# A streaming encoder layer on 8 cores: another order of loads in the head, and w_o and w_pgate loaded in pairs

## The chip, the cores and the metric
The kernel runs on all 8 cores of one Trainium2 chip, each with its own prompt sequence and its own share of the sample streams, with no exchange between cores. The time is the device time of the slowest core, in microseconds, as the median of several runs.

## The reference, cut to what matters
```python
h = rmsnorm(x, g_pre)
xa, ba, ca, za, xb, zb, ga, gb = split(h @ w_in)          # 8 sections of 1024 columns
conv = conv_b + sum(conv_w[k] * shifted(ca * xa, k) for k in range(3))
ya = ((ba * conv) * silu(za)) @ w_a_out
d  = trailing_mean(xb) - xb                               # windows 2, 4, 8, 16, by channel group
yb = ((d @ w_grp) * pool_scale * silu(zb)) @ w_b_out
m  = sigmoid(ga) * ya + sigmoid(gb) * yb
x1 = x + rmsnorm(m @ w_o, g_post)
out = x1 + (p @ w_ple) * sigmoid(x1 @ w_pgate)
```
D is 1024. A core has 2176 rows: 2048 of one prompt and 128 of four sample streams. The last rows of ca * xa and of xb are returned as well.

## The kernel before, in words
The rows are cut in tiles of 128. The first half H1 is tiles 0 to 7 (two blocks of 512 rows), the second half H2 is tiles 8 to 16 (two blocks of 512 and the sample block of 128). Each half passes through three stages.

In the first stage (P1) j runs over eight groups of 128 channels. For each j and block `p1_conv` makes four projections (xa, ca, ba, za) and `p1_pool` two (xb, zb). One projection of a block, a group (line 604), is eight matmuls of 128x128 weights against 512 columns of the transposed normed rows, which lie in hA for H1 and in hB for H2. The xb weight is multiplied with w_grp beforehand (`fold`, line 745), from a transposed copy w_xbt, two j at a time (jp). In the second stage (P2, `p2_unit`) each j and block needs four groups: ga and gb from hA or hB, then w_a_out times vT, then w_b_out times qT; their combination m goes to mT by an addition on GpSimd (line 811). The third stage (P3, `p3_tile`) multiplies tiles of m by w_o and of x1 by w_pgate; H1's P3 tiles run within H2's first stage.

Weights come from HBM in float32 and are written as bfloat16 by loads that GpSimd issues (line 595, the POOL queue), 524 KB read and 256 KB written each. They use six slots w of their own and, during H1's first stage, nine more in mT (called mT in the profile). x tiles are loaded by SyncE (lines 908 and 552, the SP queue), 512 KB each, into slots which lie in the later homes of w_o and w_pgate (called wo and wpg in the profile). In the head the SP queue holds x0, the row g_pre (line 909), x1 to x3, the small tensor sml, and x4 to x7. The POOL queue holds four weights of j = 0, four of j = 1 (after tile 0's power), two w_xbt tiles and w_grp, the fifth weights of j = 0 and 1, and the next w_xbt tiles.

A loaded x tile in the head is squared and summed on ScalarE (line 555), scaled (line 557), raised to -1/2 on GpSimd (line 559), multiplied by the statistic and g_pre on VectorE in two halves (line 562, tile hb), transposed by eight TensorE matmuls (line 575) and copied into hA (line 579). g_pre is broadcast over the partitions by two float32 matmuls with a matrix of ones (line 912), from a row in vT that is cleared ahead (line 468), and copied to gbc (line 914). While it has nothing to do in the head, TensorE multiplies the identity by itself (line 491, the filler), up to a planned 12.5 us. For j = 0 the projections of a block run tile by tile, 128 columns each; for j = 1 a block at once.

w_o and w_pgate are sixteen loads by GpSimd (line 1017), after all norms of both halves, since they overwrite the x slots. They have no slot to wait for.

What sets the order: the program records operations with an engine, a duration, a key and their dependences. `Plan.schedule` simulates the engines and the two DMA queues with these durations and the constant DMA_RATE, and takes on each engine, at each moment, the ready operation of the lowest key. From this comes a fixed order of instructions on every engine, in which each instruction waits for its semaphores. On the chip a waiting instruction holds up all that stand behind it on its engine.

## Time and profile before
| | |
|---|---|
| median of 3 runs | 759.61 us (759.2 to 760.65) |
| the profiled execution | 759.77 us |
| its span on the slowest core | 758.2 us (other cores from 756.5) |
| TensorE busy | 745.3 us, 98% |
| VectorE / ScalarE / GpSimd busy | 384.3 / 254.3 / 339.8 us |
| HBM read / written | 117.35 / 11.36 MB |

The span is from the first to the last instruction of a core. A busy TensorE is one on which a matmul is in flight, whether it is useful work or filler. DMA issues are listed by the engine that issues them, with the time from issue to landing.

### The profile page before, as it was taken

How to read it: one execution, taken by the hardware profiler on the slowest of the kernel's cores; microseconds unless marked ns; L12 is line 12 of the kernel's file. 1: busy time of each engine (PE TensorE's matmuls, PEld its weight loads, DVE VectorE, ACT ScalarE, POOL GpSimd, SP SyncE). 2: the span in 40 equal slices, each digit the busy share in tenths (PEclk: the TensorE clock that was granted, in tenths of full speed). 3: DMA queues.
4: the chain of work that ended last, by engine and by line, in shares of the span. 5: the costliest groups of instructions: out<-in, count | busy, mean ns of one | idle time of the engine just before them, and what ended most of it. 6: DMA issues, size and time to landing. Idle time of an engine off the chain costs nothing.

```text
span 758.2 us, 13217 instructions; the slowest of 8 cores (756.5 to 758.2 us)
## 1 busy us (share of the span) xinstructions
PE 745.3 (98%) x4386; PEld 376.5 (50%) x4386; DVE 384.3 (51%) x639; ACT 254.3 (34%) x514; POOL 339.8 (45%) x514
## 2 busy tenths in 40 slices
PE   6899999999999999999999999999999999999998
PEld 5665454444444444454545545455455555555444
DVE  4775667776622112455557666575751212224655
ACT  3533444442211111333333333343421111115453
POOL 5333555558642433342435536466582342211544
PEclk9999999999999999999999999999999999999999
DMA  8999769858995564827547384474747354306643
GB/s 184 219 149 195 92 156 167 155 109 130 172 156 78 75 92 61 139 76 138 87 85 129 78 135 79 90 132 63 152 84 119 56 80 63 55 0 202 157 119 125
DMA packets 65907, 87.82 MB, mean 116 GB/s; under 512 B 30897, under 2 KB 34737, under 8 KB 65842
## 3 DMA queue, kind: packets, MB, share of 16 engines
q0 software_dynamic: 29792, 50.41, 45.1%
q1 hardware_dynamic: 36050, 36.57, 17.4%
...
HBM read 117.35 MB, written 11.36 MB: 170 GB/s over the span
## 4 chain that ended last, share of the span: by engine, by line
PE 93%; DMA 4%; POOL 1%; DVE 1%; issue 1%; ACT 0%; SPq 0%; DVEq 0%; ACTq 0%; POOLq 0%
PE ps L604 74%; PE ps L829 8%; PE ps L876 7%; DMA w<-w_in 2%; PE ps L882 2%; DMA wo<-x 2%; PE ps L745 1%; PE ps L575 0%; PE ps L781 0%; POOL sp L713 0%; POOL mT L595 0%; DVE hb L562 0%; DVE sg L894 0%; ACT hb L555 0%; DVE qT L897 0%
## 5 line engine op out<-in xcount | busy, mean ns | idle before, releaser
L604 PE MATMUL ps<-hB,w 128*128 128x512 bf16 (+1 forms) x912 | 156.5, 326 | 0.0
L604 PE MATMUL ps<-hA,w 128*128 128x512 bf16 (+1 forms) x816 | 143.6, 329 | 2.6 <-DVE hA L579 1.9
L604 PEld LDWEIGHTS ps<-hB,w 128*128 128x128 bf16 x912 | 77.1, 98 | 72.0
L604 PE MATMUL ps<-hB,hA 128*128 128x512 bf16 (+1 forms) x624 | 108.6, 326 | 0.0
L604 PEld LDWEIGHTS ps<-hA,w 128*128 128x128 bf16 x816 | 69.2, 98 | 69.0 <-issue 3.7
L808 DVE SCALAR_TENSOR_TENSOR tA<-tA,ps 128x512 f32<-128x512 f32 (+1 forms) x40 | 24.3, 609 | 141.5 <-PE ps L604 141.5
L604 PE MATMUL ps<-hA,mT 128*128 128x512 bf16 x400 | 91.4, 379 | 0.0
L811 POOL TENSOR_TENSOR mT<-tA,tB 128x512 bf16<-128x512 f32 (+1 forms) x40 | 44.0, 1109 | 84.4 <-DVE tB L808 84.0
L604 PEld LDWEIGHTS ps<-hB,hA 128*128 128x128 bf16 x624 | 52.8, 98 | 49.1
L805 ACT ACTIVATE tA<-ps 128x512 f32<-128x512 f32 (+1 forms) x40 | 21.3, 533 | 152.3 <-PE ps L604 147.5
L876 PE MATMUL ps<-wpg,x1T 128*128 128x512 bf16 (+2 forms) x296 | 61.7, 362 | 0.0
L713 POOL TENSOR_TENSOR sp<-sp 128x524 f32<-128x524 f32 (+5 forms) x60 | 59.5, 992 | 4.8 <-DVE U L658 1.0
L604 PEld LDWEIGHTS ps<-hA,mT 128*128 128x128 bf16 x400 | 38.7, 98 | 45.4 <-issue 0.4
L829 PE MATMUL ps<-wo,mT 128*128 128x512 bf16 x272 | 60.8, 379 | 0.0
L604 PE MATMUL ps<-qT,w 128*128 128x512 bf16 (+1 forms) x272 | 56.4, 351 | 0.0
L699 POOL COPY X<-ptail 128x15 f32<-128x15 f32 x32 | 10.4, 325 | 98.5 <-PE ps L604 98.5
L595 POOL DMA_DIRECT2D w<-w_in x75 | 41.4, 553 | 28.0 <-PE ps L604 24.3
L713 POOL TENSOR_TENSOR sp<-X 128x526 f32<-128x526 f32 (+1 forms) x40 | 42.3, 1058 | 20.6 <-ACT X L701 20.3
L670 ACT ACTIVATE tB<-U,sml 128x512 f32<-128x512 f32 (+1 forms) x40 | 29.9, 749 | 62.2 <-DVE U L661 58.9
L604 PE MATMUL ps<-vT,w 128*128 128x512 bf16 (+1 forms) x224 | 47.8, 356 | 0.0
L876 PEld LDWEIGHTS ps<-wpg,x1T 128*128 128x128 bf16 x296 | 28.3, 98 | 30.5
L829 PEld LDWEIGHTS ps<-wo,mT 128*128 128x128 bf16 x272 | 26.6, 98 | 31.8
...
## 6 DMA issues: line engine op xcount, KB each, us to landing
w<-w_in POOLq DMA_DIRECT2D x75, 256.0 KB, 7.3
hA<-w_in POOLq DMA_DIRECT2D x26, 256.0 KB, 8.0
hA<-x SPq DMA_DIRECT2D x10, 512.0 KB, 3.5
y<-hA SPq DMA_DIRECT2D x10, 512.0 KB, 3.8
mT<-w_in POOLq DMA_DIRECT2D x19, 256.0 KB, 8.7
wo<-x SPq DMA_DIRECT2D x9, 512.0 KB, 8.2
wpg<-x SPq DMA_DIRECT2D x8, 512.0 KB, 13.9
w<-w_b_out POOLq DMA_DIRECT2D x14, 256.0 KB, 5.5
```

Source lines behind the costliest of these rows:

```text
L595: w_op = OP('pool', lambda e, d: d(e.dma_start(out=w.ap[:], in_=src)), 0.56, key, ins=list(rd), opens=[w], dma=mb, after=after, tag=name, ...
L604: ins_ = e.matmul(bk.ap[:, parts[0]:parts[1]], lhsT=w.ap[:, kk, :], rhs=act(kk), start=(kk == 0), stop=(kk == 7))
L670: OP('act', lambda e, d: d(e.activation(out=cv(), in_=win(U.ap, k, 2, 2, 2 + Es), func=AF.Identity, bias=cw(3), scale=cw(2))), act_us(N, 2 ...
L699: OP('pool', lambda e, d: d(e.tensor_copy(out=X.ap[:, 1:16], in_=ptail[:, j, :])), 0.24, ke - 1.0, ins=[tx], opens=[X], after=[gops[0]], t ...
L713: d(e.tensor_tensor(out=win(nxt.ap, k, 16, nlo, E), in0=win(cur.ap, k, 16, nlo, E), in1=win(cur.ap, k, 16, nlo - w, E - w), op=ALU.add))
L745: ins = e.matmul(bk.ap[:, i * 128:(i + 1) * 128], lhsT=wt[cb].ap[:, kk, :], rhs=wgrp[:, jp, cb, c * 128:(c + 1) * 128], start=(cb == 0), s ...
L805: OP('act', lambda e, d, t=t, g=g: d(e.activation(out=t.ap[:, 0:N], in_=bks[g].ap[:, 0:N], func=AF.Tanh, scale=0.5)), act_us(N), ke + g8 * ...
L808: OP('dve', lambda e, d, g=g: d(e.scalar_tensor_tensor(out=tt[g].ap[:, 0:N], in0=tt[g].ap[:, 0:N], scalar=1.0, in1=bks[2 + g].ap[:, 0:N], ...
L811: OP('pool', lambda e, d: d(e.tensor_tensor(out=mT[:, j, k.rel:k.rel + N], in0=tt[0].ap[:, 0:N], in1=tt[1].ap[:, 0:N], op=ALU.add)), pool_ ...
L829: ins = e.matmul(ob[h].ap[:], lhsT=mT[:, kk, tl.rel:tl.rel + 128], rhs=wo[:, kk, h * 512:(h + 1) * 512], start=(kk == 0), stop=(kk == 7))
L876: ins = e.matmul(bg.ap[:, 0:n], lhsT=x1T.ap[:, kk, :], rhs=wpg[:, kk, sl], start=(kk == 0), stop=(kk == 7))
L882: ins = e.matmul(be.ap[:, 0:n], lhsT=pT.ap[:, kk, :], rhs=wple[:, kk, sl], start=(kk == 0), stop=(kk == 1))
```

## The change
The head's loads get another order. The SP queue holds x0, g_pre, x1 to x4; the eight weights of j = 0 and 1 are issued after x1 has landed; x5 to x7 after the second weight of j = 1; the w_xbt tiles after x5. Block 1 of H1 is cut for the convolutions of j = 0 and 1 into tile 4 and tiles 5 to 7. The order by keys is: block 0 with j = 0 tile by tile, block 0 with j = 1, tile 4 with both j, tiles 5 to 7 with both j (tile by tile for j = 0). The copies into hA in the head move from VectorE to ScalarE, and hb is made in one instruction of 1024 columns but for tile 0. The memsets of vT and of ones shrink to one row of ones, and the broadcast matmuls use that one row. The filler is one matmul of 512 columns instead of four of 128. The two buffers of the fold are taken with the w_grp load. Each pair of w_o and w_pgate chunks of step j in H1's second stage waits for the last group of step j - 1 of block 0. The planner's DMA rate depends on the time.

```diff
-DMA_RATE = 0.30
+DMA_RATE = ((0.0, 0.36), (4.4, 0.20), (7.0, 0.33), (46.0, 0.30))
...
-        OP('dve', lambda e, d: d(e.memset(vT_[:].bitcast(F32)[:, 0:1024], 0.0)), 0.6, -60.0, outs=[res("vT_reg")], tag='grow0')
-        OP('dve', lambda e, d: d(e.memset(ones[:], 0.0)), 0.2, -47.0, outs=[res("ones")], tag='ones')
-        OP('dve', lambda e, d: d(e.memset(ones[0:1, :], 1.0)), 0.1, -46.9, ins=[res("ones")], outs=[res("ones")], tag='ones1')
+        OP('dve', lambda e, d: d(e.memset(ones[0:1, :], 1.0)), 0.1, -47.0, outs=[res("ones")], tag='ones')
...
-                for _ in range(n):
-                    ins = e.matmul(wb.ap[:, 0:128], lhsT=ident_b[:], rhs=ident_b[:], start=True, stop=True)
+                d(e.matmul(wb.ap[:, 0:n * 128].rearrange("p (a c) -> p a c", a=n), lhsT=ident_b[:], rhs=ident_b[:].unsqueeze(1).broadcast_to([128, n, 128]),
+                           start=True, stop=True))
...
-            for h in range(2):
+            pk = -60.0 + gi if gi < 8 else key + 0.3
+            cols = ((0, 512), (512, 1024)) if gi == 0 else ((0, 1024),)
+            for c0, c1 in cols:
...
+                if ev == 'act':
+                    OP('act', lambda e, d: d(e.copy(out=hv[:, :, tl.rel:tl.rel + 128], in_=tb.ap[:].bitcast(BF16).rearrange("p (k c) -> p k c", k=8))),
+                       0.9, key + 0.6, ins=[tb], outs=[hreg(tl)], tag=f'ev{gi}')
...
-            OP('pe', lambda e, d, h=h: d(e.matmul(gb[h].ap[:], lhsT=ones[:], rhs=grow[:, h * 512:(h + 1) * 512], start=True, stop=True)),
+            OP('pe', lambda e, d, h=h: d(e.matmul(gb[h].ap[:], lhsT=ones[0:1, :], rhs=grow[0:1, h * 512:(h + 1) * 512], start=True, stop=True)),
...
-        for n, tl in enumerate(H1.tiles[:4]):
-            norm(tl, -20.0 + n, -38.0 + n + (1.0 if n else -1.5), True, loaded=(x0, x0_load) if n == 0 else None)
+        for n, tl in enumerate(H1.tiles[:5]):
+            norm(tl, -20.0 + n, -38.0 + n + (1.0 if n else -1.5), True, loaded=(x0, x0_load) if n == 0 else None, ev='act', hbs=[p_hb, p_hq] if n > 2 else None)
...
+            wf = [Buf(pools, f'wf{jp}{c}') for c in range(2)]
...
-        load_secs(0, 0, -32.0, [p_w, p_wm], (0, 1, 2, 3))
-        load_secs(0, 1, -22.0, [p_w, p_wm], (0, 1, 2, 3), [H1.tiles[0].pow])
-        for n, tl in enumerate(H1.tiles[4:]):
-            norm(tl, -10.0 + n, -32.0 + n, True, hbs=[p_hq])
-        wt = load_wt(0, -14.0, [p_w, p_wm])
+        load_secs(0, 0, -32.0, [p_w, p_wm], (0, 1, 2, 3), [H1.tiles[1].load])
+        load_secs(0, 1, -22.0, [p_w, p_wm], (0, 1, 2, 3))
+        for n, tl in enumerate(H1.tiles[5:]):
+            norm(tl, -10.0 + n, -32.0 + n, True, hbs=[p_hq, p_hb], load_after=[w_ops[(0, 1, 1)]], ev='act')
+        wt, wf = load_wt(0, -14.0, [p_w, p_wm], [H1.tiles[5].load])
...
-        for j in range(2):
-            for k in H1.blocks:
-                p1_conv(j, k, wins[(0, 1, j)], kp + (2 * j + k.b) * 4 * G8 + (6.0 if k.b else 0.0), j == 0)
+        b0 = H1.blocks[0]
+        parts = []
+        for lo, hi in ((4, 5), (5, 8)):
+            k = Blk()
+            k.half, k.b, k.samp, k.N, k.rel, k.tiles = 0, 1, False, (hi - lo) * 128, lo * 128, H1.tiles[lo:hi]
+            parts.append(k)
+        p1_conv(0, b0, wins[(0, 1, 0)], kp, (0, 1, 2, 3))
+        p1_conv(1, b0, wins[(0, 1, 1)], kp + 4 * G8, None)
+        for j in range(2):
+            p1_conv(j, parts[0], wins[(0, 1, j)], kp + 8 * G8 + j * G8, None)
+        for j in range(2):
+            p1_conv(j, parts[1], wins[(0, 1, j)], kp + 10 * G8 + 3 * j * G8, (0, 1, 2) if j == 0 else None)
...
+        p2_done = []
...
-                   outs=[res(f"{name}{kk}")], dma=0.524, sem=f"ld_{name}{kk}", after=norm_done, tag=f'{name}{kk}')
+                   outs=[res(f"{name}{kk}")], dma=0.524, sem=f"ld_{name}{kk}", after=norm_done + p2_done[-1:], tag=f'{name}{kk}')
...
+            p2_done.append(H1.blocks[0].p2v[-1])
```

## Rows read from the trace of the kernel before
**Rows 1.** Table of stretches: start:end, length, busy us (count) by engine, granted clock, DMA.
```profile
0.00:25.82 25.82, 17.21 (x201) 13.68 (x202) 11.91 (x23) 8.26 (x16) 14.38 (x59) 1.00 0.94 200
25.82:213.56 187.74, 187.74 (x1120) 94.82 (x1120) 126.25 (x205) 73.49 (x132) 100.24 (x150) 1.00 0.88 152
213.56:214.30 0.74, 0.00 (x2) 0.03 (x1) 0.00 (x0) 0.59 (x1) 0.18 (x1) 1.00 0.96 139
214.30:751.00 536.70, 536.70 (x3027) 264.72 (x3028) 242.59 (x402) 170.26 (x363) 223.65 (x304) 1.00 0.53 98
```
**Rows 2.** Chain of waits in order of time: start us, us, what.
```profile
2.34 0.30 SPq L909
3.11 13.02 DMA wo<-x
38.24 0.89 PE ps L604 x16
46.22 1.73 PE ps L604 x8
...
197.08 17.08 DMA w<-w_in
```
**Rows 3.** TensorE up to 25.82 by line and form: count, busy, mean ns, idle before.
```profile
L604 PE MATMUL ps<-hA,w 128*128 128x128 bf16 x97 | 6.5, 219 | 1.9 <-DVE hA L579 1.9
L575 PE MATMUL ps<-ident_b,hb 128*128 128x128 bf16 x32 | 2.4, 218 | 2.3 <-DVE hb L562 1.3 <-DVE U L658 1.0
```
**Rows 4.** DMA issues of 0 to 1.5, 0 to 21 and 20.1 to 20.7: median landing.
```profile
wo<-x SPq DMA_DIRECT2D x1, 512.0 KB, 4.1
...
w<-w_in POOLq DMA_DIRECT2D x6, 256.0 KB, 12.1
mT<-w_in POOLq DMA_DIRECT2D x5, 256.0 KB, 21.4
mT<-w_xbt POOLq DMA_DIRECT2D x4, 256.0 KB, 22.3
...
mT<-w_in POOLq DMA_DIRECT2D x1, 256.0 KB, 23.4
```
**Rows 5.** Timeline of ScalarE and VectorE in the head; last, VectorE's hb by form.
```profile
16.20 1.06 ACT L555 ACTIVATE hb<-wo 128x1024 bf16<-128x1024 f32 x1 [2.39 <-DMA wo<-x]
33.83 1.06 ACT L555 ACTIVATE qT<-wpg 128x1024 bf16<-128x1024 f32 x1 [0.72 <-DMA wpg<-x]
...
13.43 0.69 DVE L579 COPY hA<-ps 128x1024 bf16<-128x1024 bf16 x1 [0.86 <-PE ps L575]
21.03 0.69 DVE L579 COPY hA<-ps 128x1024 bf16<-128x1024 bf16 x1 [0.86 <-PE ps L575]
...
L562 DVE SCALAR_TENSOR_TENSOR hb<-wo,stats,gbc 128x512 bf16<-128x512 f32 x8 | 6.0, 752 | 2.7 <-POOL stats L559 2.1 <-DVE gbc L914 0.2
```
**Rows 6.** Loads issued at 193, 248, 250 to landing; GpSimd and TensorE timeline around them.
```profile
w<-w_in POOLq DMA_DIRECT2D x1, 256.0 KB, 16.4
w<-w_a_out POOLq DMA_DIRECT2D x1, 256.0 KB, 3.8
w<-w_b_out POOLq DMA_DIRECT2D x1, 256.0 KB, 5.4
...
193.56 1.06 POOL L1017 DMA_DIRECT2D wpg<-w_pgate  x2
247.81 0.57 POOL L595 DMA_DIRECT2D w<-w_a_out  x1
249.54 0.53 POOL L595 DMA_DIRECT2D w<-w_b_out  x1 [1.16 <-PE ps L604]
257.46 1.89 PE L604 MATMUL ps<-qT,w 128*128 128x512 bf16 x8
```
**Rows 7.** Filler matmuls (line 491) up to 6.5 and from 6.5 to 12.7: ns min/median/max.
```profile
L491 PE MATMUL ps<-ident_b x24: 266/314/314, 3.7 to 6.1; 128*128 128x128 bf16 x24
...
L491 PE MATMUL ps<-ident_b x32: 219/219/314, 10.7 to 12.6; 128*128 128x128 bf16 x32
```

More of the change, by code:

```diff
@@ L28, with dma_rate @@
 MM = 0.2157
+def dma_rate(t):
+    return [r for t0, r in DMA_RATE if t0 <= t + 1e-9][-1]
 def mm_us(n):
@@ L222, in ring_step @@
                     return
-                rate = DMA_RATE / len(heads)
-                end = min([dma_t + r[0][1] / rate for r in heads] + nxt + [t])
+                rate = dma_rate(dma_t) / len(heads)
+                end = min([dma_t + r[0][1] / rate for r in heads] + nxt + [t] + [t0 for t0, _ in DMA_RATE if t0 > dma_t + 1e-9])
                 for r in heads:
@@ L238, in ring_next @@
             if heads:
-                rate = DMA_RATE / len(heads)
-                return min([dma_t + r[0][1] / rate for r in heads] + nxt)
+                rate = dma_rate(dma_t) / len(heads)
+                return min([dma_t + r[0][1] / rate for r in heads] + nxt + [t0 for t0, _ in DMA_RATE if t0 > dma_t + 1e-9])
             return min(nxt) if nxt else None
@@ L542, in build_program, with norm @@
         early_tr = []
[L544 removed]
+        def norm(tl, key, key_load, pe_tr, load_after=(), hbs=None, hold=0.0, loaded=None, ev='dve'):
             gi = tl.gi
@@ L631, in p1_groups @@
             if tilewise:
-                for n, tl in enumerate(k.tiles):
+                for n in tilewise:
+                    end = min([c for c in tilewise if c > n] + [len(k.tiles)])
                     for i, g in enumerate(gs):
-                        c0 = n * 128
-                        go = group(key + 1.73 * max(i, n) + 0.1 * n + 0.01 * i, bks[i], 128, (c0, c0 + 128), ws[g],
-                                   lambda kk, tl=tl: hv[:, kk, tl.rel:tl.rel + 128], [ws[g], hreg(tl)], n == 0, f'p1t_{j}_{k.b}_{g}_{n}')
+                        c0, c1 = n * 128, end * 128
+                        go = group(key + 1.73 * max(i, n) + 0.1 * n + 0.01 * i, bks[i], c1 - c0, (c0, c1), ws[g],
+                                   lambda kk, c0=c0, c1=c1: hv[:, kk, k.rel + c0:k.rel + c1], [ws[g]] + [hreg(t) for t in k.tiles[n:end]], n == 0, f'p1t_{j}_{k.rel // 128}_{g}_{n}')
                         gops.append(go)
@@ L689, in p1_pool @@
             W = WINS[jp]
-            (b_xb, b_zb), gops = p1_groups(j, k, ws, key, False, (5, 4))
+            (b_xb, b_zb), gops = p1_groups(j, k, ws, key, None, (5, 4))
             g8 = 8 * mm_us(N)
@@ L730, in p1_pool, with fold @@
                dve_us(N), ke + 1.9, ins=[sw, zb, res("sml")], outs=[areg("q", j, k)], after=early_tr if j >= 6 and k.half == 0 else (), tag='q2')
-        def fold(jp, wt, key, pools):
-            ws = []
+        def fold(jp, wt, ws, key):
             for c in range(2):
-                w = Buf(pools, f"wf{jp}{c}")
+                w = ws[c]
                 for hh in range(2):
@@ L941, in load_secs, with load_wt @@
                 ws[g], w_ops[(half, j, g)] = load_w(blkw(w_in, SECS[g] * 8 + j), key + 1.5 * g, pools, f'w{half}{j}{g}', after)
-        def load_wt(jp, key, pools):
+        def load_wt(jp, key, pools, after=()):
             wt = []
+            wf = [Buf(pools, f'wf{jp}{c}') for c in range(2)]
             for cb in range(2):
-                w, o = load_w(w_xbt[(2 * jp + cb) * 128:(2 * jp + cb + 1) * 128, :].rearrange("p (k c) -> p k c", k=8), key + 0.1 * cb, pools, f't{jp}{cb}')
+                w, o = load_w(w_xbt[(2 * jp + cb) * 128:(2 * jp + cb + 1) * 128, :].rearrange("p (k c) -> p k c", k=8), key + 0.1 * cb, pools, f't{jp}{cb}', after)
                 wt.append(w)
             o = OP('pool', lambda e, d: d(e.dma_start(out=wgrp[:, jp, :, :], in_=w_grp[jp * 256:(jp + 1) * 256, :].rearrange("(k p) c -> p k c", k=2))), 0.6,
-                   key + 0.3, outs=[res(f"wgrp{jp}")], dma=0.26, sem=f"ld_wgrp{jp}", tag='ldwgrp', seq='w')
-            return wt
+                   key + 0.3, outs=[res(f"wgrp{jp}")], opens=wf, dma=0.26, sem=f"ld_wgrp{jp}", tag='ldwgrp', seq='w')
+            return wt, wf
         def load_p2(half, j, key, pools):
@@ L987, in build_program @@
             pools = [p_w, p_wm] if jp < 3 else [p_wm, p_w]
-            wt = load_wt(jp, (kp - 42.0) if jp > 1 else -8.0, pools)
+            wt, wf = load_wt(jp, (kp - 42.0) if jp > 1 else -8.0, pools)
             for j in (2 * jp, 2 * jp + 1):
@@ L991, in build_program @@
                 load_secs(0, j, (kj - 40.0) if j > 2 else -6.0, pools, (0, 1, 2, 3, 4))
-            wf = fold(jp, wt, kp - 4.0, pools)
+            fold(jp, wt, wf, kp - 4.0)
             for j in (2 * jp, 2 * jp + 1):
```

28 lines of the change are left out of this document (12 added, 16 removed).

## The prediction
> **What bounds the kernel now.** I read the table of stretches first. TensorE is idle 8.61 us of the first 25.82 (25.82 - 17.21), then not at all up to 213.56, 0.74 us from there to 214.30, and not again until 751.00, at full granted clock throughout [rows 1]. So a change elsewhere moves the time only if it moves one of three things: what is lost ahead of 25.82, the 0.74, or the 7.2 us after the last full stretch, which no edit touches. The chain of waits names the first two. It holds one DMA of x tiles for 13.02 us from 3.11, and one DMA of a w_in tile for 17.08 us from 197.08 to 214.16, just ahead of the 0.74 [rows 2]. DVE, ACT and POOL have slack in every long stretch and are left aside.
>
> The idle time alone understates what the head loses, since the filling matmuls count as busy. I count useful work instead. Before 25.82 TensorE did 96 of the 128-column projections (97 are listed, the last begins at 25.82) and four tile transposes [rows 3]. At 0.89/16 = 0.0556 us a matmul of 128 columns [rows 2], eight of them, 0.45 us, for a transposed tile, that is 5.34 + 1.80 = 7.1 us. **The head loses 25.8 - 7.1 = 18.7 us**; after it nothing is lost but the 0.74.
>
> **Transport in the head, before.** Eight x tiles and, up to the issue at 20.22, fifteen weight-sized loads (6 + 5 + 4) and two w_grp loads of half that size (load_wt, twice) are in flight, 24 equal transfers [rows 4]. The first lands at 1.06 + 4.1 = 5.2 us, the last at 20.22 + 23.4 = 43.6 [rows 4]. That is 38.4/23 = 1.67 us each, so transfer n lands near 3.5 + 1.67n. Check: by POOL landings between them x7 is about the 18th, 33.6; ACT gets it at 33.83 [rows 5]. Since both queues share this rate, the x tiles come as late as they do because weights for section 4, the fold and j = 1 come between them.
>
> **The new head, step by step.** (a) x0 to x4 go alone at first, landing at 5.2, 6.8, 8.5, 10.2; the POOL queue waits for x1, so the first weight is issued near 7 and shares with x4: both are there at n = 6, 13.5. (b) The eight weights follow, 15.2, 16.9, 18.5, 20.2, 21.9, 23.5, 25.2. (c) x5 waits for the sixth weight (21.9), is issued, and overlaps the last one: 14th, 26.9. x6 28.5, x7 30.2, or 31 with the first w_xbt load beside it (released by x5). So x7 comes some 3 us earlier than now.
>
> (d) A landed tile takes 5.5 us to stand in hA: 16.20 to 21.03 + 0.69 [rows 5]. ACT now does the evacuation; the trace has no such copy. Its bounds are DVE's 0.69 and ACT's 1.06 for the same 128x1024 elements plus 0.2; I take 1.06, the same engine and size [rows 5]. The two halves of hb in one instruction: between nothing and 0.2 us saved, I take 0. Latency 5.7-5.9. ACT carries at least 2 x 1.06 = 2.1 us a tile (square and evacuation), more than the 1.67 between landings, but tiles 1 to 4 are squared while tile 0 waits for the g_pre row; behind it DVE's hb (two halves of 0.752, 1.5 us) [rows 5] paces them, so I let them follow 1.1 to 1.6 us apart.
>
> (e) Tile 0 is ready at 13.43 + 0.69 = 14.1 now [rows 5], held by the g_pre broadcast. The dropped vT memset is what the g_pre issue at 2.34 waits for [rows 2]; x0's issue at 1.06 [rows 4] is over near 1.5, so it goes out 0.8 to 0.9 us earlier, and no weight stands ahead of it. I take 0.9 and add 0.4 for ACT: 13.6. Less could be had if its landing is set otherwise (nothing, 14.5), more if it lands with x0 (12.6). Ones as one row: same columns, nothing. The filler as one 512-column matmul: same columns, nothing, off the chain. So tile 0 and weight 0 meet at 13.6; tiles 1 to 4 at about 15.1, 16.2, 17.4, 19.
>
> (f) TensorE then does one group at 13.6, and from 15.1 it has work without a break, because each weight now feeds four or five tiles (5 x 0.445 = 2.2 us) and comes every 1.67. Useful work by 15.1: two transposes and a group, 1.35. **Loss 15.1 - 1.35 = 13.8 us.** Tiles 0 to 4 with eight weights are 40 x 0.445 + 5 x 0.45 = 20.0 us, which last until 33.8; tile 5 is ready at 26.9 + 5.8 = 32.7, tile 6 at 34.4, tile 7 at 36.8, against needs at 33.8, 36.0 and 38.3. No new gap, by a margin of 1.1 to 1.6 us. Splitting block 1 in 128 and 384 columns adds 32 matmuls of 128 columns net, 0.1 us. The head gains 18.7 - 13.8 - 0.1 = **4.8 us**.
>
> The Trainium skill, "DMA: Bandwidth & Descriptors", section "Where 436 GB/s comes from", puts HBM at about 358 GB/s for a core, an estimate of 1.46 us for 524 KB; 14 transfers would be 2.9 us earlier. The trace shows 1.67, and I keep it.
>
> (g) **w_o and w_pgate two by two.** Now these loads stand ahead of weights in the POOL queue: the w_in load of 193.00 took 16.4 us to land, and the one of 197.08 17.08 us, with two w_pgate loads between [rows 6, 2]. With two per step in place of all sixteen ahead, the 17 us fall well under 10, while only 0.74 is late: **0.74 us** gone. Next late there is nothing in view, since the later second-stage steps wait for nothing [rows 1]. What is added: a POOL wait for the q group of the step before, ahead of each pair. Behind it on POOL stand the m addition (needs the same group) and the next step's weights (need a later one), so the wait itself costs nothing. The pairs' transfers do come ahead of those weights. The w_b_out load at 249.54 lands 5.4 us later, at 254.9, and its group starts at 257.46 [rows 6]: 2.5 us to spare. In the queue of 193 to 197 a load takes (214.16 - 209.4)/3 = 1.6 us. A pair issued near 245.5 begins to land 3.8 us later, 249.3, and the fourth load behind it (w_b_out) lands at 249.3 + 3 x 1.6 = 254.1. Cost nothing; other end in the third rival. w_pgate's last pair goes out near 280, 30 us before it is read.
>
> (h) The fold's two buffers are now taken with the w_grp load, so 14 of 15 weight slots are bound per pair of j. The j = 2 weights wait for j = 0 slots, free near 38, and have until j = 0 and 1 are through, 45.5 + 64 fold matmuls of 0.0556 + eight groups of 1.73, about 63: nothing, at most 1 us. The new rates in the planner reorder work that has slack: between -0.3 and +0.3, I take 0.
>
> **Sum.** The profiled execution took 759.77 (span 758.2). 759.77 - 4.8 - 0.74 = 754.2. The median of the runs is 0.16 below that execution: **754.1**.
>
> **The rivals.**
> 1. The stream is slower with ordered loads, 2.0 us a transfer. For it: w_b_out lands 3.3 us after w_a_out with no queue before it [rows 6], so the stream can be slower than 1.67; against it: 1.67 is the mean over 24 in this stretch. Then tile 7 stands at 3.5 + 32 + 5.8 = 41.3, and j = 0 and 1 end at 41.3 + 1.8 + 5.2 = 48.3, where they end now at 25.8 + (31.6 - 7.1) = 50.3 (31.6 = 256 x 0.0556 + 8 groups of 1.73 + 8 x 0.45; 5.2 is four groups of three tiles). Gain 2.0 + 0.74: 756.9. Chance 0.12.
> 2. Tile 0 leads: g_pre lands with x0 and transfers take 1.5. Start 12.6, loss about 11.8, gain 6.9 + 0.74: 752.0. Chance 0.12.
> 3. **The other side.** The pairs make w_b_out late in each of seven steps. For it: that 3.3 (249.54 + 5.4 less 247.81 + 3.8) [rows 6]. With 3.3 in place of 1.6 a load it would land at 249.3 + 9.9 = 259.2, 1.7 us late, seven times: 12 us, 766. It decides from 2.7 us a load on ((257.46 - 249.3)/3). Against it: that same stream passes loads at 1.6 when they stand in line. Chance 0.07.
> 4. The clock. The 24 fillers that begin at 3.7 have a median of 314 ns, the 32 from 10.7 on 219 [rows 7]: the lower of the two levels (1.2 GHz) while TensorE had just begun, 2.4 GHz after it had been busy, though the table gives 1.00 for the whole stretch [rows 1]. In the new head TensorE does little between the fillers' end near 12.5 and 15.1. If it fell back for as long as the lower level can have lasted at the start (3.7 to 10.7), 7 us would pass at half speed, 3.5 us lost: 757.6. Against it: the present head has 1.9 + 2.3 us of idle before these groups and transposes, and their mean is still 218 and 219 ns [rows 3]. Chance 0.04. The Trainium skill, "TensorE: Matmul & The Clock Gate", section "What's actually happening", says that the idle array is gated to the lower clock; by that rule this rival would come true if the pause counts as idle; the trace agrees for the time before the first matmuls and has no second such pause.
>
> **How the numbers follow.** Forecast 0.65 (own range 753.2 to 755.3), rivals 0.12, 0.12, 0.07, 0.04. The range 751.7 to 757.9 leaves out most of the third rival and the outer ends of the others. A measurement tells 0.2%, 1.5 us, from no change. Faster: 0.65 + 0.12 + 0.11 + 0.02 and less for what no case foresees: 0.87. Slower 0.07, same 0.06.
>
> **What would show it.** In the trace after: ACT gets x1 near 7 and x4 near 13.5; first w lands near 13.5; TensorE has no gap from about 15 on; x7 reaches ACT near 31 (33.83 now); the convolution groups of j = 0 and 1 are over near 45.5 (50.3 now); no wait at the second stage's start; last matmul 5.5 us earlier. I am wrong if tile 5 is waited for near 33, if w_a_out or w_b_out ends a TensorE wait between 215 and 300, or if groups after 13 take twice 0.0556 us a matmul.

## The result and the profile after

The changed kernel took **767.41 us** (median of four runs, 765.44 to 769.79) against 759.95 for the kernel before beside it; the ratio is 1.010, 95% interval 1.0084 to 1.0116. I had forecast 754.1 and a range up to 757.9: the sign was wrong.

The profiled execution took 765.44 us, 5.67 more than that of before, with a span of 763.8 on core 6 (cores 759.6 to 763.8). The median lies 2.0 above it: in the two slowest of the four runs core 4 took 767.5 and 768.3 us, where it took 760.6 in the profiled one. These runs left no trace, so their extra time stays open, and what follows explains the 765.44. First its table of stretches, to set beside [rows 1]; I cut it where TensorE's state changes.

```profile
0.00:21.20 21.20, 16.71 (x125) 9.04 (x126) 9.00 (x15) 12.33 (x21) 9.98 (x51) 1.00 0.91 194
21.20:34.53 13.33, 13.32 (x147) 9.38 (x144) 5.45 (x11) 6.92 (x12) 2.96 (x6) 1.00 0.78 171
34.53:37.65 3.12, 0.01 (x1) 0.04 (x2) 2.59 (x5) 1.89 (x7) 3.10 (x4) 1.00 1.04 140
37.65:40.00 2.35, 2.35 (x31) 2.35 (x32) 2.35 (x3) 1.18 (x2) 0.20 (x1) 0.71 1.09 124
40.00:42.00 2.00, 2.00 (x22) 2.00 (x20) 1.30 (x5) 1.55 (x3) 0.00 (x0) 0.50 1.09 187
42.00:44.00 2.00, 2.00 (x38) 2.00 (x37) 1.16 (x5) 1.37 (x3) 0.00 (x0) 0.99 0.81 151
...
217.30:752.40 535.10, 535.00 (x3018) 263.68 (x3017) 242.58 (x401) 170.45 (x362) 230.28 (x316) 1.00 0.58 104
```

Three things are to be seen. TensorE works without a break from 21.20, where I had said 15.1. Then it stands for 3.12 us, and behind that gap its granted clock (the column before the DMA share) is 0.71 and 0.50, the lower of the two levels, for some 4 us. After 44 the long stretches are as full as they were.

I count the head as in the prediction. Up to 21.15 these are the projections (L610) and the transposes (L577), by count, busy us and mean ns:

```profile
L610 PE MATMUL ps<-hA,w 128*128 128x128 bf16 x64 | 4.2, 219 | 0.9 <-DMA w<-w_in 0.4 <-ACT hA L582 0.4
L577 PE MATMUL ps<-ident_b,hb 128*128 128x128 bf16 x32 | 2.5, 223 | 1.4 <-DVE hb L564 1.4
L577 PE MATMUL ps<-ident_b,vT 128*128 128x128 bf16 x8 | 0.6, 219 | 0.0
```

That is 64 projection matmuls and five transposed tiles, 3.56 + 2.25 = 5.8 us of useful work: a loss of 15.4. The gap is 3.1. The clock takes 2.35 x 0.29 + 2.00 x 0.50 = 1.7. **Together 20.2 us where before lost 18.7: the head is 1.5 us slower, not 4.8 faster.** The 0.74 us at 213.56 is gone, and 0.2 stands in its place, so TensorE should end 1.5 - 0.74 + 0.2 = 1.0 later. The last groups, after and then before (start, us):

```profile
752.40 3.68 PE L880 MATMUL ps<-wpg,x1T 128*128 128x256 bf16 x40
```
```profile
750.98 3.68 PE L876 MATMUL ps<-wpg,x1T 128*128 128x256 bf16 x40
```

The end is 1.4 later: 0.1 more is the splitting of block 1, 0.1 the idle time in the last stretch, and 0.2 stays open.

The head doesn't lose on every core. In order of the time at which ScalarE gets tile 5 (us):

| core | gets x5 | TensorE's gap behind it | last group begins | before |
|---|---|---|---|---|
| 2 | 28.17 | 0.37 | 748.73 | 750.98 |
| 1 | 28.48 | 0.26 | 748.22 | 749.40 |
| 4 | 29.53 | 1.47 | 749.18 | 749.26 |
| 5 | 29.59 | 2.04 | 751.03 | 750.67 |
| 7 | 30.09 | 2.41 | 751.32 | 750.08 |
| 0 | 30.11 | 2.68 | 752.36 | 750.93 |
| 3 | 30.73 | 3.10 | 751.45 | 749.57 |
| 6 | 31.10 | 3.12 | 752.40 | 750.80 |

The later tile 5, the longer the gap, but for 0.1 us between the first two. Where the gap is small, TensorE ends 1.2 to 2.3 us earlier than before; the time is that of the slowest core.

The remaining 4 us lie behind the last matmul. These are the closing DRAINs of GpSimd (POOLq) and SyncE (SPq): duration in ns, then start in us; before first, then after.

```profile
L387 POOLq DRAIN  x1: 4975/4975/4975, 751.5 to 751.5; - x1
L387 SPq DRAIN  x1: 13/13/13, 758.0 to 758.0; - x1
```
```profile
L391 POOLq DRAIN  x1: 10374/10374/10374, 753.2 to 753.2; - x1
L391 SPq DRAIN  x1: 13/13/13, 759.6 to 759.6; - x1
```

Before, GpSimd's DRAIN ended at 751.5 + 5.0 = 756.5, under the last stores, which end at 758.0. Now it ends at 753.2 + 10.4 = 763.6, 4.0 us after the stores' 759.6. All eight cores show this, 4.97 to 4.98 before and 10.36 to 10.37 after.

**Why the gap.** The chain of waits of the head (start, us, what), against [rows 2]:

```profile
12.10 11.78 DMA w<-w_in
...
23.95 7.07 DMA wpg<-x
...
31.56 1.11 POOL mT L601 x2
32.66 0.62 POOL wgrp L953
...
33.36 1.09 POOL mT L601 x2
...
34.46 1.06 POOL stats L560
```

x5 is issued at 23.95, behind the sixth weight, and lands at 31.02. Its arrival also releases five loads on GpSimd, and these stand ahead of its own pow (L560), which starts at 34.46. The timelines of ACT, DVE and TensorE around it:

```profile
31.10 1.06 ACT L556 ACTIVATE vT<-wpg 128x1024 bf16<-128x1024 f32 x1 [3.76 <-DMA wpg<-x]
32.16 0.80 ACT L677 ACTIVATE tB<-U,sml 128x512 f32<-128x512 f32 x1
38.34 1.01 ACT L582 COPY hA<-ps 128x1024 bf16<-128x1024 bf16 x1 [1.92 <-PE ps L577]
...
33.06 0.75 DVE L679 SCALAR_TENSOR_TENSOR tB<-U,sml,tB 128x512 f32<-128x512 f32 x1 [3.19 <-ACT tB L677]
35.61 1.28 DVE L564 SCALAR_TENSOR_TENSOR vT<-wpg,stats,gbc 128x1024 bf16<-128x1024 f32 x1 [0.53 <-POOL stats L560]
36.81 0.68 DVE L683 TENSOR_TENSOR tB<-ps,tB 128x512 f32<-128x512 f32 x1
37.42 0.16 DVE L665 COPY U<-tails 128x2 f32<-128x2 f32 x1
...
15.40 1.06 PE L610 MATMUL ps<-hA,w 128*128 128x128 bf16 x16
21.20 7.19 PE L610 MATMUL ps<-hA,w 128*128 128x128 bf16 x80
31.68 2.84 PE L610 MATMUL ps<-hA,w 128*128 128x128 bf16 x48
37.65 0.61 PE L577 MATMUL ps<-ident_b,vT 128*128 128x128 bf16 x8 [3.12 <-DVE U L665]
```

ACT stands 3.76 us at the square of tile 5. Behind it in its order waits the first elementwise step of another tile group (L677), DVE stands 3.19 us for that, and the DVE read of PSUM at 36.81 comes late with it. TensorE's next transposes start at 37.65, and the copy of tile 5 (L582) ends at 39.35.

**The stream.** In the table of stretches (last columns: clock, DMA share, GB/s) the DMA engines are nearly idle just then, on core 6:

```profile
30.00:32.00 2.00, 2.00 (x15) 1.06 (x14) 0.00 (x0) 0.90 (x1) 0.44 (x1) 1.00 0.34 125
32.00:34.00 2.00, 2.00 (x40) 2.00 (x38) 0.75 (x1) 2.00 (x6) 2.00 (x5) 1.00 0.21 26
```

**The second stage.** Before, the load in the chain here was one of w_in of 17.08 us [rows 2]. On core 6 it is now one of w_b_out of 8.17, and the w_in loads issued behind it take 8.3 and 7.7.

```profile
208.87 8.17 DMA w<-w_b_out
```

On core 0 TensorE waits later, for a w_a_out that is issued at 220.85 behind w_ple (215.80) and a pair (218.55):

```profile
229.49 1.89 PE L610 MATMUL ps<-vT,w 128*128 128x512 bf16 x8 [1.13 <-DMA w<-w_a_out]
```

### The profile page after: what moved, and what is told of

It is laid out like the page before. It is cut to its first block, busy times and chain, and to the rows that moved or that the text cites. A ratio compares the mean times of both kernels' runs of the same rounds, so it can differ in the third digit from the quotient of the medians.

```text
span 763.8 us, 13221 instructions; the slowest of 8 cores (759.6 to 763.8 us)
## 1 busy us (share of the span) xinstructions
PE 746.1 (98%) x4367; PEld 376.3 (49%) x4367; DVE 373.1 (49%) x627; ACT 261.9 (34%) x528; POOL 342.6 (45%) x514
## 4 chain that ended last, share of the span: by engine, by line
PE 92%; DMA 4%; POOL 1%; issue 1%; DVE 0%; ACT 0%; DVEq 0%; ACTq 0%; POOLq 0%; SPq 0%
PE ps L610 74%; PE ps L833 8%; PE ps L880 7%; PE ps L886 2%; DMA w<-w_in 2%; DMA w<-w_a_out 1%; PE ps L751 1%; DMA wpg<-x 1%; DMA wo<-x 1%; POOL w L601 0%; PE ps L785 0%; POOL mT L601 0%; PE ps L577 0%; POOL stats L560 0%; DVE qT L901 0%
## 5 line engine op out<-in xcount | busy, mean ns | idle before, releaser
L610 PE MATMUL ps<-hB,w 128*128 128x512 bf16 (+1 forms) x912 | 156.5, 326 | 0.0
L610 PE MATMUL ps<-hA,w 128*128 128x512 bf16 (+2 forms) x784 | 131.5, 322 | 0.4 <-DMA w<-w_in 0.2
L610 PEld LDWEIGHTS ps<-hB,w 128*128 128x128 bf16 x912 | 77.1, 98 | 72.0
L610 PE MATMUL ps<-hB,hA 128*128 128x512 bf16 (+1 forms) x624 | 108.6, 326 | 0.0
L610 PE MATMUL ps<-hA,mT 128*128 128x512 bf16 (+2 forms) x464 | 101.5, 375 | 0.0
L610 PEld LDWEIGHTS ps<-hA,w 128*128 128x128 bf16 x784 | 65.4, 98 | 60.1 <-issue 0.9
L610 PEld LDWEIGHTS ps<-hB,hA 128*128 128x128 bf16 x624 | 52.8, 98 | 49.1
L610 PEld LDWEIGHTS ps<-hA,mT 128*128 128x128 bf16 x464 | 45.4, 100 | 50.7
L610 PE MATMUL ps<-qT,w 128*128 128x512 bf16 (+1 forms) x272 | 56.6, 351 | 0.0
L720 POOL TENSOR_TENSOR sp<-X 128x526 f32<-128x526 f32 (+1 forms) x40 | 44.1, 1104 | 20.8 <-ACT X L708 20.5
L601 POOL DMA_DIRECT2D w<-w_in x70 | 38.7, 555 | 31.7 <-PE ps L610 28.0
L677 ACT ACTIVATE tB<-U,sml 128x512 f32<-128x512 f32 (+2 forms) x42 | 30.7, 731 | 63.5 <-DVE U L668 58.7
L610 PE MATMUL ps<-vT,w 128*128 128x512 bf16 (+1 forms) x224 | 47.8, 356 | 1.1 <-DMA w<-w_a_out 1.1
```

The source lines that it names most:

```text
L601: w_op = OP('pool', lambda e, d: d(e.dma_start(out=w.ap[:], in_=src)), 0.56, key, ins=list(rd), opens=[w], dma=mb, after=after, tag=name, ...
L610: ins_ = e.matmul(bk.ap[:, parts[0]:parts[1]], lhsT=w.ap[:, kk, :], rhs=act(kk), start=(kk == 0), stop=(kk == 7))
L677: OP('act', lambda e, d: d(e.activation(out=cv(), in_=win(U.ap, k, 2, 2, 2 + Es), func=AF.Identity, bias=cw(3), scale=cw(2))), act_us(N, 2 ...
L720: d(e.tensor_tensor(out=win(nxt.ap, k, 16, nlo, E), in0=win(cur.ap, k, 16, nlo, E), in1=win(cur.ap, k, 16, nlo - w, E - w), op=ALU.add))
```

## The experiments

Ratios are to the kernel before on the same chip, intervals 95%. "The base" is the changed kernel without the pairs. 4 to 7 and 9 were timed once and have no interval; they are read for the length of GpSimd's DRAIN, which is the same to 0.01 us on all eight cores of each profiled kernel.

**1. The base.** The gate on the w_o and w_pgate loads goes back to what it was:

```diff
-                   ..., after=norm_done + p2_done[-1:], tag=f'{name}{kk}')
+                   ..., after=norm_done, tag=f'{name}{kk}')
```

> The changed kernel with w_o and w_pgate loaded as before, all sixteen at once (the wait for the step before taken off, nothing else). Theory A, the loss is in the head and in the long GpSimd drain at the end, neither of which the pairs touch: the time stays at that of the changed kernel, 765 to 769 us, the last matmul near 756, and the TensorE wait of 1.2 us or less at the start of the second stage becomes one of 0.7 or more. Theory B, the pairs are what costs: the time falls to 760 or below. The drain on GpSimd, 10.4 us in the changed kernel and 5.0 before, is read in either case.

Measured: 1.0024 (1.0014 to 1.0034), +1.8 us, median 762.04; GpSimd's DRAIN 4.98 us. So neither theory held as it was put: the head loses by itself, and it has nothing to do with the long DRAIN.

By cores the base falls in two groups. Cores 1, 3, 5 and 7 take 755.4 to 757.3 us, where no core took less than 756.5 before; cores 0, 2, 4 and 6 take 759.9 to 761.5. All four of these stand still for 1.8 to 2.7 us near 41 or 42 and run at the lower clock behind it, as core 2 here (TensorE's timeline, then two stretches; clock, DMA share and GB/s last). "issue" means that the profile shows nothing that was waited for.

```profile
42.42 5.82 PE L610 MATMUL ps<-hA,w 128*128 128x128 bf16 x65 [1.83 <-issue]
...
42.00:44.00 2.00, 1.58 (x16) 1.58 (x16) 0.82 (x3) 0.00 (x0) 0.00 (x0) 0.60 0.55 102
44.00:46.00 2.00, 2.00 (x23) 2.00 (x22) 0.00 (x0) 0.00 (x0) 0.00 (x0) 0.55 0.01 2
```

Core 7 has the stop (1.84) without the lower clock and takes 757.3; cores 1, 3 and 5 have no such stop. Tile 5 costs the eight cores 1.6 us of waiting at most. So in the base this second stop, and the clock behind it, decide the time. On core 2 one 16 KB transfer of the DMA queue that the profile calls "instruction" lies between 40.1 and 41.4, just ahead of its end. Whether TensorE waits for that is not shown, and no experiment here is aimed at it.

**2. The pairs alone**, on the kernel before (`p2_done` and the gate, nothing else).

> The kernel before with the pairs alone: each pair of w_o and w_pgate chunks waits for the step before, nothing else changed. Theory A: the head is that of before, the wait of 0.74 us at 213.56 goes or halves, so 759.2 to 759.9 us if the drain on GpSimd stays at 5.0 us; about 763 if the pairs are what makes the drain 10.4 us. Theory B, the pairs cost: 762 or more with waits for w_a_out or w_b_out between 215 and 300.

Measured: 1.0063 (1.0046 to 1.0079), +4.8 us. GpSimd's DRAIN takes 10.37 us. TensorE on core 0:

```profile
230.15 1.89 PE L604 MATMUL ps<-vT,w 128*128 128x512 bf16 x8 [1.84 <-DMA w<-w_a_out]
```

With 1.8 of the head this is 6.6 of the 7.5 us. The pairs bring the long DRAIN, and near 229 a wait for w_a_out of 0.5 to 1.8 us on four cores, on core 0 more than the 0.74 they remove.

**3. Fewer instructions on GpSimd.** The changed kernel with 14 memsets less (one memset fills invcnt for the window of 16, so the first rows of that window's groups are scaled otherwise).

> The changed kernel with 14 instructions fewer on GpSimd, 919 in place of 933 (before has 923): the count table for the window of 16 is filled by one memset with 1/16, so the first 15 rows of the last channel groups come out scaled wrongly. Theory C, the drain at the end depends on how many instructions GpSimd has run, with a step between 923 and 933: drain 5.0 us and the time 3 to 4 us below the changed kernel's, about 763. Theory D, the drain depends on something else (order of the loads, what is in flight): 10.4 us and no difference in time.

Measured: 1.007 (1.0048 to 1.0092), DRAIN 10.36. The number of instructions is not it. The counterpart, ten memsets more on the kernel before, was never timed.

**4. and 5. Pairs only in the last steps; pairs gated by a DMA.**

```diff
+  after=norm_done + (p2_done[-1:] if j >= 5 else [])      # 4
+  after=norm_done + [w_last]                              # 5
```

> The kernel before with the wait on the step before for the last three pairs alone (steps 5, 6, 7), the first ten chunks all at once. Theory E, the drain grows with the number of GpSimd loads that wait for TensorE in the second stage: between 5.0 and 10.4 us, near 7. Theory F, it takes one of two values, by where the last loads of a long queue stand: 5.0 or 10.4 us exactly.

> The kernel before with each pair waiting for the last weight load of its own step and not for a TensorE group, so spread over the second stage all the same. Theory G, the spreading is what makes the drain long: 10.4 us, span 762 to 764 us. Theory H, the wait on TensorE's semaphore is: 5.0 us, span near 758 us.

Measured: 763.84 with a DRAIN of 10.37, and 764.49 with 10.53 (before: 761.03). In the first TensorE ended between 753.7 and 754.9, as before, so the whole loss is the DRAIN; and it doesn't matter whether the gate is TensorE or a DMA.

**6. More loads.** The kernel before with four more GpSimd loads of 64 KB into a scratch tile.

> The kernel before with four GpSimd loads of 64 KB more (rows of p to a scratch tile that nothing reads) after the norms, 210 loads in place of 206. Theory I, the drain goes by where the queue's ring stands at the end, so by the number of loads: a value other than 5.0 us. Theory J, it doesn't: 5.0 us. The head and TensorE's end stay as they are, span 758 us with a drain of 5.0, 762 with 10.4.

Measured: 761.18, DRAIN 4.98.

**7. and 8. The place of w_ple**, the one larger load: ahead of the sixteen in one run; or in the fifth step, with the pairs.

> The kernel before, all sixteen w_o and w_pgate loads in one run, but the w_ple load (twice the size of the others) issued ahead of them: it is GpSimd's load number 55 of 206, where it was number 83. This tells two theories of the longer closing DRAIN of GpSimd apart. Theory S (the spreading of the sixteen loads, or that the last of them come late, makes it 10.4 us): DRAIN 4.98 us, time 759 to 761.5. Theory P (the place of the w_ple load among the 206 makes it: 83 and 87 gave 4.98, 69 and 75 gave 10.4): DRAIN about 10.4, time about 763.5 to 765.

> The kernel before with the loads of w_o and w_pgate two by two, as in the changed kernel, but w_ple loaded in the fifth step of the second stage and not in the second: it is GpSimd's load number 89. Theory S (spreading): DRAIN 10.4 us and a time near 765, as with the pairs alone. Theory P (place of w_ple): DRAIN 4.98 us, and the time is that of the kernel before, within 1 us, since the pairs cost at most some 1 us of wait at the start of the second stage and give back 0.74 us.

Measured: DRAIN 4.97 and 10.36. Theory P fell both times. The first took 766.25 all the same, with no long DRAIN: with one more large load ahead of the weights TensorE waits 2.4 to 4.4 us for w_in on each core. The second: 1.0054 (1.0037 to 1.007). In it no core waits for a load between 217 and 240 us; w_a_out is late near 271 instead, by 0.9 to 2.1 us on five cores, in the step that now has both w_ple and a pair ahead of it.

**9. All sixteen in one run, but late**, after a group of the fourth step:

```diff
-            for name, dst, src, kk in rl[2 * j:2 * j + 2]:
+            for name, dst, src, kk in (rl if j == 4 else []):
```

> The kernel before, with all sixteen w_o and w_pgate loads in one run as before, but only after the q group of the fourth step of the second stage has run: they are GpSimd's loads 75 to 94, the last ones some 9 loads earlier than with the pairs (103). w_ple is load 65. If the lateness of the last w_pgate loads makes the closing DRAIN longer: 10.4 us. If their being spread over eight steps does: 4.98 us. The pairs where only the last six were spread (loads 90 to 103) gave 10.4.

Measured: 779.58. Core 0:

```profile
L387 POOLq DRAIN  x1: 10613/10613/10613, 767.2 to 767.2; - x1
```

and its waits:

```profile
PE ps L604 <- DMA w<-w_a_out: 12.7, 1, 12.7
```

So the spreading isn't needed; being late is enough. Where the sixteen loads meet weights that are needed soon, they cost 12 us.

**10. Tile 5 released earlier**, on the base: x5 to x7 wait for the fourth weight and not for the sixth.

```diff
-  load_after=[w_ops[(0, 1, 1)]], ev='act')
+  load_after=[w_ops[(0, 0, 3)]], ev='act')
```

> The changed kernel without the pairs (762.0 us), with x5 to x7 issued once the fourth weight of j = 0 has landed and not the sixth. Theory A, the late x5 is what the new head loses by: on the slowest core x5 reaches ScalarE at 31 us, ScalarE, VectorE and the PSUM banks stand still behind it, and the clock falls after the gap. Then x5 comes 3 to 4 us earlier, the TensorE gap near 35 (up to 3 us) and the low clock behind it go, and the time is 756 to 758 us. Rival B, the same bytes only change places: the weights of j = 1 come later by as much, TensorE waits for them between 20 and 30 us instead, 761 to 762 us.

Measured: 1.0049 (1.0034 to 1.0064), above the base's 1.0024 (the intervals touch). x5, issued some 3 us sooner, landed no sooner: at 28.4 to 30.0 over the eight cores, and at 27.6 to 29.9 in the base. That is rival B. On core 7, the slowest, ACT got x5 at 29.64, the gap was still 2.0 us, weights were waited for, and the stop that shows no cause was 2.9 us:

```profile
PE ps L577 <- issue: 2.9, 1, 2.9
...
PE ps L577 <- DVE U L665: 2.0, 1, 2.0
PE ps L610 <- DMA w<-w_in: 1.9, 4, 0.8
```

**11. ACT's order**, on the base: the planner reckons with less transport from 20 to 32 us and writes the convolution's steps ahead of tile 5's square.

```diff
-DMA_RATE = ((0.0, 0.36), (4.4, 0.20), (7.0, 0.33), (46.0, 0.30))
+DMA_RATE = ((0.0, 0.36), (4.4, 0.20), (7.0, 0.33), (20.0, 0.22), (32.0, 0.30))
```

> The changed kernel without the pairs, with one number of its planner altered: from 20 to 32 us it reckons with 0.22 MB/us in place of 0.33. No load is moved in kind; ACT's written order now has the copies and activations of j = 1, tiles 0 to 3, ahead of the square of tile 5, in place of behind it. Theory Q (the late tile 5 does harm because in-order ACT holds the convolution's elementwise work of other tiles behind its square, so that PSUM banks come free late): the gap near 37 us is gone or under 1 us, the clock doesn't fall after it, and the time is 1.5 to 3 us less than with the changed kernel without the pairs, 759 to 760.5. Theory R (the loads themselves are late: whatever the order, TensorE waits for tile 5): a gap of 1 us or more stands before tile 5's transposes or projections, and the time stays at 762 or within 0.5 us of it.

Measured: 1.0017 (1.0006 to 1.0029), against 1.0024 of the base: the intervals overlap. The wait for L665 is gone; waits for tile 5 itself and the next tiles took its place, 2.8 and 1.5 us on core 0:

```profile
PE ps L577 <- DVE hb L564: 2.8, 2, 1.5
...
PE ps L577 <- DVE vT L564: 1.5, 1, 1.5
```

So the order on ACT cost nothing that can be told apart: with it gone, a tile that is late anyway is waited for. Theory R held.

**12. x5 to x7 one after the other**, on the base.

```diff
-  load_after=[w_ops[(0, 1, 1)]], ev='act')
+  load_after=[w_ops[(0, 1, 1)]] if n == 0 else [H1.tiles[4 + n].load], ev='act')
```

> The changed kernel without the pairs, where x6 is issued when x5 has landed and x7 when x6 has; x5 is issued as before, behind the sixth weight. Theory S (the three x tiles, issued together, share the stream, so that x5 lands 7 us after its issue and only 1 us before x6): x5 alone lands 3 to 4 us after its issue, near 27 to 28, TensorE's wait before tile 5's transposes falls by 2 us or more; x6 and x7 then land near 30.5 and 34. Theory T (x5 is late because of the weights and w_xbt loads ahead of and beside it): it still takes 6 us or more. The time itself I expect between 761 and 764, since x7 comes no earlier.

Measured: 1.0037 (1.0026 to 1.0048). On core 2 x5, alone on its queue, took 4.3 us, where in the base, issued with x6 and x7, it took 5.9 (the others 6.9 and 7.6). But that core is the base's worst: over all eight x5 takes 4.1 to 4.8 us alone, 4.5 in the mean, and 3.8 to 5.9 in the base, 4.8 in the mean. Theory S is not borne out beyond 0.3 us. ACT got x5 at 28.76 on core 2, 1.2 us earlier than the base's 29.97, and x7 at 43.54 (base: 32.96):

```profile
28.76 1.06 ACT L556 ACTIVATE vT<-wpg 128x1024 bf16<-128x1024 f32 x1 [1.13 <-DMA wpg<-x]
```

and in the waits of that core:

```profile
PE ps L577 <- issue: 3.3, 1, 3.3
PE ps L577 <- DVE hb L564: 3.3, 2, 1.8
```

**13. No gates on the head's loads**, on the base: weights don't wait for x1, nor x5 to x7 for a weight, nor w_xbt for x5.

```diff
-  (0, 1, 2, 3), [H1.tiles[1].load])
+  (0, 1, 2, 3))
-  load_after=[w_ops[(0, 1, 1)]], ev='act')
+  ev='act')
-  load_wt(0, -14.0, [p_w, p_wm], [H1.tiles[5].load])
+  load_wt(0, -14.0, [p_w, p_wm])
```

> The changed kernel without the pairs, and with the three gates on its head's loads removed: the weights don't wait for x1, x5 to x7 don't wait for the sixth weight, the first w_xbt loads don't wait for x5. Tiles and groups are computed as in the new head. Theory G (the gates cost: they leave the last x tiles to the end of the stream, behind all weights): x5 reaches ACT before 29, the gap of 1 to 3 us near 37 us goes, and the time falls by 1.5 us or more against the changed kernel without the pairs, to 760 or less. Theory T (the total transport decides: sixteen loads at about 1.8 us each end near 32 in any order): x5 comes earlier, but the weights later, TensorE waits for w_in for 1 to 4 us instead, and the time stays within 1 us of 762.

Measured: 0.9997 (0.9987 to 1.0006), 2 us better than the base. On core 0 the stream never stands (DMA share, the last column but one), the clock stays at 1.00, and TensorE waits for weights instead:

```profile
30.00:32.00 2.00, 2.00 (x23) 1.41 (x22) 2.00 (x3) 1.42 (x4) 1.05 (x1) 1.00 1.09 168
```

Its waits:

```profile
PE ps L610 <- DMA w<-w_in: 3.1, 3, 1.3
PE ps L610 <- issue: 1.9, 1, 1.9
```

ACT took x5 at 25.89 to 26.63 on the eight cores. The gain is as theory G had it, the waits for w_in are those of theory T: the three gates together cost 2 us, and without them the new head is as fast as the old one, not faster.

**14. Only the w_xbt gate removed**, on the base.

> The changed kernel without the pairs, with one gate removed: the first two w_xbt loads, w_grp and the fifth weights of j = 0 and 1 don't wait for x5. x5 to x7 still wait for the sixth weight. Theory I (the idle stream of 30 to 34 us costs: what comes later comes later by it): the DMA share stays near 1.0 there, the waits on w_in go, and the time falls by 1 us or more against the changed kernel without the pairs (ratio to before 1.001 or less). Theory L (the late tiles 5 to 7 cost, and more loads beside them make them later still): x5 reaches ACT at 31 or later, x7 at 36 or later, TensorE waits longer for hb, the clock falls, and the time rises above that of the changed kernel without the pairs (ratio 1.003 or more).

Measured: 1.0028 (1.0015 to 1.004), between the bounds of the two theories and not to be told from the base's 1.0024. Filling the idle stream gained nothing, against theory I. The signs are those of theory L: with w_xbt loads beside them the last x tiles come later still, on core 0 x5 at 34.17 and x7 at 40.50, and TensorE waits 3.3 us and then runs at the lower clock:

```profile
34.17 1.06 ACT L556 ACTIVATE vT<-wpg 128x1024 bf16<-128x1024 f32 x1 [3.85 <-DMA wpg<-x]
```

The wait:

```profile
PE ps L577 <- DVE vT L564: 3.3, 1, 3.3
```

And a stretch behind it (clock, DMA share and GB/s last):

```profile
38.00:40.00 2.00, 1.94 (x19) 1.97 (x20) 0.98 (x5) 2.00 (x6) 0.54 (x1) 0.50 0.88 183
```

**15. The small parts alone**, on the kernel before: no vT memset, ones as one row, the fillers joined.

> The kernel before with three small parts of the changed head alone: no memset of the vT buffer ahead of the g_pre load, ones as one row, the filling matmuls as one of 512 columns. Order of loads and tiles is as before. My prediction's step (e) priced the earlier g_pre row at 0.9 us. Theory 1 (tile 0 is held by the g_pre broadcast, and the loads' order sets the rest): tile 0 is ready 0.5 to 0.9 us earlier, but the weights and x4 to x7 come when they came, so the time is 759.5 to 760.3, the same. Theory 2 (the row's earliness is worth its whole 0.9): 759.1 or less. With DRAIN 4.98 us in both.

Measured: **0.9981 (0.9971 to 0.999)**, 1.4 us faster, median 759.65 against 761.15, which beats both kernels. This is theory 2: its price of 0.9 us lies in the interval, 0.8 to 2.2 us. In the timeline of TensorE the 48 matmuls that begin at 25.82 before begin at 24.96 (its x47 is one record short), and the waits for hb and U of 1.3 and 1.0 us on core 2 are down to 0.3:

```profile
24.96 5.40 PE L600 MATMUL ps<-hA,w 128*128 128x128 bf16 x47 [0.50 <-DVE hA L575]
```

**16. With them, ACT's copies and the joined hb**, loads as before.

```diff
-  OP('dve', lambda e, d: d(e.tensor_copy(out=hv[:, :, tl.rel:tl.rel + 128], ...
+  OP('act', lambda e, d: d(e.copy(out=hv[:, :, tl.rel:tl.rel + 128], ...
```

> The kernel before, its order of loads kept, with the three small parts (no vT memset, ones as one row, joined filling matmuls), and in addition the placement of work of the new head: the transposed head tiles are copied to hA by ACT and not by DVE, and hb is one instruction of 1024 columns except for tile 0 (the stores of wfold have a semaphore each, which moves nothing). The three small parts alone took 0.19% off. Theory A (in-order ACT, now also with the copies, holds the convolutions back): slower than the small parts alone, 760.5 or more. Theory O (the order of the loads alone is to blame): as the small parts alone or up to 1 us faster, 758.7 to 760.

Measured: 0.9983 (0.9972 to 0.9994), the same as 15. The placement of this work neither gains nor loses. What loses is in the rest of the new head, some 3 us against the base: the order and the gates of the loads, the cut of block 1, the fold's buffers and the planner's rates. Experiment 13 puts 2 us of it on the gates; the others were not tried one by one.

**17. The small parts, and the sixteen loads four by four in the first four steps.**

> The kernel before with the three small parts of the head and with w_o and w_pgate four by four in the first four steps of the second stage, each but the first four after the q group of the step before. Closing DRAIN: if its length turns between the 75th and the 94th load, I can't say on which side 90 lies; nearest is 94, so 10.4 us. With 10.4 the time is 762 to 764, with 4.98 it is that of the small parts alone less up to 0.7 (758.5 to 760). Rival: four loads ahead of a step's weights make w_a_out or w_b_out late in steps 1 to 3 by 1 to 3 us each, and the time is above 764.

Measured: 0.9987 (0.9977 to 0.9997), no better than 15. DRAIN 4.24, the shortest of all, where I had expected 10.4:

```profile
L387 POOLq DRAIN  x1: 4241/4241/4241, 750.8 to 750.8; - x1
```

Put together, by the time at which GpSimd issues the last w_pgate load: in the profiled kernels where it is at 191 to 200 us, the DRAIN is 4.97 to 4.98; here, at 238.5, 4.24; in 9, where the last eight go out from 253.4 to 257.7, 10.61; where it is at 287.7 to 297.1 (2, 4, 5, 8 and the changed kernel), 10.36 to 10.53. The length goes with how late these loads are issued, and takes a step somewhere between 239 and 258 us. Their time and their place among GpSimd's loads (90th, 94th) move together here and aren't told apart. What GpSimd does in it, and why a load some 460 us before the end matters, no run shows; that stays open.

## Why the prediction was wrong

The forecast for the profiled execution was 754.2, and it took 765.44: 11.2 us. By its own steps:

**(a), (b) The first tiles and weights: 1.6 us off at the start.** x1 landed at 8.06 and not at 6.8. The first weight, which waits for it, was issued at 8.66 and took 6.5 us beside x2 to x4: there at 15.2 and not 13.5. Step (e) was right, tile 0 stood in hA at 12.53 + 0.99 = 13.5 (forecast 13.6), but it met no weight. The first group ran at 15.40, unbroken work began at 21.20, and the loss up to there was 15.4 in place of 13.8. Counted as in the prediction, the sixteen transfers from x0 (4.86) to x7 (33.57) are 1.91 us apart, near the 2.0 of my first rival (chance 0.12); the eight weights in a row are 1.60 apart (15.17 to 26.39). So it is the mixed transfers that were put too fast.

**(c) The step that failed most.** x5 was put at 26.9 and landed at 31.02. Half of that is the sixth weight, at 23.87 in place of 21.9: the delay of (a) and (b), handed on by the gate. The other half is x5's own transfer, 7.07 us in place of 5.0. This one is not the same on every core: it took 4.7 us on cores 1 and 2, 5.6 to 6.1 on five others, and 7.07 on core 6, so that x5 landed between 28.1 and 31.0. I had reckoned with one mean rate and one core, and the slowest core sets the time. What makes the transfer longer on one core than on another no run shows; that x6 and x7 go out beside it explains little (experiment 12).

**(d) The latency, 5.7 to 5.9 us,** became 8.3 for tile 5 (31.02 to 38.34 + 1.01, the end of its copy). I hadn't seen that x5's landing releases five loads ahead of its own pow on GpSimd: 34.46 - 33.14, 1.3 us, the mean square being ready at 32.86 + 0.28. The rest is ACT and DVE behind the late square. Need was 34.53, ready 39.35: "no new gap, by a margin of 1.1 to 1.6" turned into a gap of 3.1 us on this core, and of 0.3 to 3.1 over the cores.

**(f) The clock,** my fourth rival, with a chance of 0.04, came true on some cores. At its own place, behind the fillers, it was low on cores 0 and 1; core 1 had 0.50 up to 18 us, and core 0:

```profile
12.00:14.00 2.00, 1.43 (x10) 0.99 (x10) 1.47 (x2) 1.62 (x4) 2.00 (x5) 0.54 1.09 138
```

This did not set the time: core 1 is the one whose last group begins first, at 748.22. On cores 0, 5, 6 and 7 the clock fell after the gap near 37, and there it costs 1.7 us on core 6. Six cores show it near there in experiment 14, none in 13 and 15. The length of a gap alone doesn't tell: core 3 stayed at 1.00 after 3.10 us, and core 5 had 0.74 and 0.50 after 2.04. I had taken the pauses of one core, about 0.9 us each, for the proof that it wouldn't fall, but core 5 of the kernel before has a pause of 2.13 us ahead of 16.59 and a clock of 0.58 and 0.57 from 17 to 21. Head in all: 1.6 + 3.1 + 1.7 = 6.4 us of the 11.2. The Trainium skill, "TensorE: Matmul & The Clock Gate", section "What's actually happening", says that an idle array is gated to the lower clock; the trace of core 6 agrees, for this gap, and core 3 shows a gap of the same length without it.

**(g) The pairs.** The mechanism was right as far as it went: the w_in loads that took 16.4 and 17.08 us take 8.3 and 7.7, and the 0.74 us wait is gone. My third rival, w_b_out late in each of seven steps, did not come. But loads are late once or twice: w_b_out by 0.2 us at 217 on core 6, and w_a_out by 0.4 to 1.1 us near 229 on cores 0, 3, 5 and 7, where w_ple and a pair stand ahead of it. When w_ple moves (experiment 8), this wait moves with it; a pair alone can do it too, for in experiment 3 core 5 waits 1.1 us near 271. I had priced it at nothing from a step 20 us further on that has no w_ple.

**The tail, "which no edit touches".** It was touched, 4.0 us of the 11.2, and neither the forecast nor a rival had it. The DRAIN of before stood in the trace with 4.98 us, 1.5 us short of the stores' end. The step that failed is that I took the 7.2 us after the last full stretch for fixed; I never asked what sets the DRAIN's length, because an engine's closing seemed to be no work. The head, this tail and the 0.2 in place of nothing are 10.6 of the 11.2 us. Nothing in the trace of before could have given 10.4 us. That its cover was only 1.5 us could have been read.

**Signs.** Of those I named, x4 (13.0) was near. The first weight, the unbroken work from 15, x7 near 31, the convolution groups over near 45.5 (52.1 on core 6), no wait at the second stage's start and a last matmul 5.5 us earlier all failed. All three alarms came: tile 5 was waited for, w_a_out and w_b_out ended waits between 215 and 300, and on cores 0 and 1 the first groups ran at the lower clock.
